# Output products that wait chunk by chunk, rotated parts first, and the context's product at the head of the second block

## The chip, the cores and the metric

The kernel runs on one core of one Trainium2 chip. The time is device microseconds of one execution. Three runs of the kernel before gave 3758.86, 3758.86 and 3766.8 us, median 3758.86 us. The profiled execution took 3765.87 us, and its span, from its first to its last instruction, 3764.2 us.

## The reference, cut to what matters

Two transformer blocks run one after the other on 256 tokens of width 1024, in fp32. The first has four layers: latent attention (layers 0 and 3), stick-breaking attention (layer 1) and retention (layer 2), each followed by a feed-forward part. The second has two layers with a context of 256 more tokens, each ending in a mixture of 64 experts.

```python
# latent attention: q has a plain part (128 per head) and a rotated part (64 per head)
q = (rms_norm(q_lat, q_norm) @ w_q_up).reshape(b, s, MLA_HEADS, MLA_NOPE + MLA_ROPE)
q = jnp.concatenate([q_nope, apply_rope(q_pe, cos, sin)], axis=-1)
kv = (rms_norm(kv_lat, kv_norm) @ w_kv_up).reshape(b, s, MLA_HEADS, MLA_NOPE + MLA_V)
k_pe = apply_rope(k_pe[:, :, None, :], cos, sin)
o = blocked_causal_softmax(q, k, v, (MLA_NOPE + MLA_ROPE) ** -0.5)
return o.reshape(b, s, MLA_HEADS * MLA_V) @ w_out
# retention: a norm, a gate, then the output product
o = o * lax.rsqrt(jnp.mean(o * o, axis=-1, keepdims=True) + EPS)
o = (jax.nn.silu(g) * (o.reshape(b, s, hv) * gn_g)) @ w_out
# second block, first layer: both sets of tokens meet the same weights
h  = x * (1.0 + sc1) + sh1
hc = ctx * (1.0 + csc1) + csh1
f, q, k, v = jnp.split(h @ w_in, cuts, axis=-1)
fc, qc, kc, vc = jnp.split(hc @ w_in, cuts, axis=-1)
```

## The kernel before, in words

Activations lie with the width on the 128 partitions, as 8 chunks of 128 rows by 256 tokens. Weights come from HBM in pieces of 1 MB through a ring of 8 slots (`ring<-stream_in`), which SyncE loads in a fixed order. A slot is given back by the first matmul on the piece behind it (`take`, `piece_used`), so the loads run up to seven pieces ahead. A second stream brings the weights of the modulation vectors (`mod_stream_in`); VectorE multiplies these itself, in L1730 and L1733. In layer 0's latent attention SyncE loads them too, each half piece when VectorE is through with the one two before it.

Each engine has its own list of instructions, written out in the program, and works it off in that order. They meet in semaphores: a PSUM bank has one for "filled" and one for "drained" (`bank`, `wait_filled`, `wait_drained`), and a table `PLAN` names the bank of each product. Nothing is reordered at run time, so an engine whose next instruction waits does nothing.

Five places matter here.

- Latent attention, `mla` (layers 0 and 3). TensorE multiplies by four groups of weights: the plain query part (8 outputs of 256 columns, L709), the key part (L817), the values (L824) and the query's rotated part (4 outputs, L709). Then a fixed matrix `rot` turns the query's rotated part (L837) and the shared key's (L840). ScalarE copies queries and values out of PSUM (L1408), VectorE the keys (L1699). The rotation itself is sine products on VectorE (L1899 to L1902), the key's sum and its two masked copies there too (L1903 to L1907), and cosine products and sums of the query on GpSimd (L2403, L2405). Attention begins when all that is done. In layer 0 VectorE has two modulation pieces between these steps, and TensorE turns their results (L721) before the first scores.
- The output products `mix_out` of latent and stick-breaking attention (`pair`, L746). Before, TensorE waits until every head's output has been copied, then multiplies.
- Retention's output product (L709). Head by head, VectorE takes a reciprocal (L1982) and multiplies four chunks by it (L1984), then GpSimd multiplies those four chunks by the gate in one instruction of 1024 columns (L2439). TensorE waits for all four heads.
- The head of the second block, `fourier_gqa`. VectorE modulates the latent tokens (L2009), GpSimd the context's (L2451). `token_major` multiplies tokens by the first weight piece: first the latent tokens, then the context's.
- `attention`, the loop over heads and query blocks, whose first score follows the wait in `mla`.

## Time and profile before

| | |
|---|---|
| median of three runs | 3758.86 us (3758.86 to 3766.8) |
| profiled execution | 3765.87 us |
| its span | 3764.2 us |
| mean granted TensorE clock | 0.953 |
| TensorE busy | 3329.9 us, 88% |
| VectorE busy | 1402.9 us, 37% |
| ScalarE busy | 504.7 us, 13% |
| GpSimd busy | 425.3 us, 11% |

The profile names an engine (PE is TensorE, DVE is VectorE, ACT is ScalarE, POOL is GpSimd, SP is SyncE), a line of the program and the tiles that an instruction writes and reads. An fp32 matmul stands as two records, so "x16" on TensorE is eight matmuls of the program. The span falls into the first block (to about 1820 us), the second block's first layer (to about 2880 us) and its second layer. A bracket at the end of a row is the time the engine sat idle before it, and the instruction that ended this.

### The profile page before, as it was taken

The numbers are of one execution on the slowest core, as the hardware profiler recorded it, in microseconds if no ns is written. First come the engines' busy times: TensorE is split into PE (matmuls) and PEld (weight loads), VectorE is DVE, ScalarE is ACT, GpSimd is POOL, SyncE is SP. The second block draws the span as 40 slices with busy tenths as digits, with TensorE's granted clock in tenths as the row PEclk, the third lists the DMA queues.
The fourth block names the chain that finished last, engine by engine and source line by source line (L and its number), as shares of the span: only waits on it lengthen the run. The fifth ranks groups of instructions, "written<-read, shape, count | busy, mean of one in ns | idle before, by whom it ended". The sixth has DMA issues, their size and how long they took to land.

```text
span 3764.2 us, 40279 instructions
## 1 busy us (share of the span) xinstructions
PE 3329.9 (88%) x14228; PEld 2238.3 (59%) x14228; DVE 1402.9 (37%) x3085; ACT 504.7 (13%) x1021; POOL 425.3 (11%) x478
## 2 busy tenths in 40 slices
PE   3799897998999997889898897999894998999998
PEld 2678785887887886778664533434442676333333
DVE  7555615565013564574363322222213033111112
ACT  1210012000011002100031211111111021111111
POOL 0010102001000000000210311111112002000000
PEclk9899999999999999999999899999997999999999
DMA  7467532774434762366200479999994214998994
GB/s 291 179 240 283 225 135 89 291 274 160 157 111 180 290 268 90 135 245 234 100 34 12 164 255 349 384 376 376 363 368 145 101 59 175 382 388 367 414 369 188
DMA packets 136152, 870.05 MB, mean 231 GB/s; under 512 B 19248, under 2 KB 22448, under 8 KB 38448
## 3 DMA queue, kind: packets, MB, share of 16 engines
q1 hardware_dynamic: 94528, 675.32, 45.5%
q0 software_dynamic: 39984, 190.35, 15.5%
q8 instruction: 100, 1.64, 0.2%
q10 hardware_dynamic: 1472, 2.18, 0.2%
q14 instruction: 68, 0.56, 0.0%
HBM read 849.95 MB, written 36.18 MB: 235 GB/s over the span
## 4 chain that ended last, share of the span: by engine, by line
PE 71%; DMA 13%; DVE 8%; issue 4%; ACT 1%; POOL 1%; SPq 0%; DVEq 0%; POOLq 0%; ACTq 0%
PE ps L709 15%; PE ps L990 12%; PE ps L1230 10%; PE ps L973 9%; DMA ring<-stream_in 9%; PE ps L746 8%; PE ps L1252 6%; PE ps L1268 3%; DMA moe_out<-arena,slot_out 2%; DMA arena<-mod_stream_in 2%; PE ps L1199 2%; PE ps L735 1%; DVE arena L1733 1%; PE ps L1167 1%; DVE YS L1835 1%
## 5 line engine op out<-in xcount | busy, mean ns | idle before, releaser
L1230 PE MATMUL ps<-ring,arena 128*64 128x512 f32 (+2 forms) x2112 | 618.0, 630 | 79.2 <-DMA ring<-stream_in 79.2
L1733 DVE SCALAR_TENSOR_TENSOR arena<-arena,cond 128x512 f32<-128x512 f32 x630 | 447.6, 748 | 72.7 <-DMA arena<-mod_stream_in 62.7
L1230 PEld LDWEIGHTS ps<-ring,arena 128*64 128x64 f32 (+2 forms) x2112 | 224.7, 157 | 413.4 <-issue 411.6
L973 PE MATMUL ps<-H,ring 128*128 128x256 f32 x2048 | 453.9, 383 | 14.3 <-ACT H L1430 14.3
L990 PE MATMUL ps<-arena,ring 128*128 128x256 f32 x2048 | 445.9, 380 | 4.3 <-DVE arena L1995 4.3
L973 PEld LDWEIGHTS ps<-H,ring 128*128 128x128 f32 x2048 | 391.8, 193 | 68.2 <-issue 15.7
L990 PEld LDWEIGHTS ps<-arena,ring 128*128 128x128 f32 x2048 | 389.4, 191 | 56.6 <-issue 5.0
L1252 PE MATMUL ps<-ring,arena 128*64 128x512 f32 (+2 forms) x1056 | 314.4, 611 | 17.3 <-DMA ring<-stream_in 9.3
L1408 ACT ACTIVATE arena<-ps 128x512 f32<-128x512 f32 (+2 forms) x359 | 182.7, 509 | 861.3 <-PE ps L709 347.5
L2201 DVE TENSOR_TENSOR arena<-arena,ps 128x256 f32<-128x256 f32 x83 | 35.0, 421 | 653.3 <-ACT arena L1627 653.3
L746 PE MATMUL ps<-H,ring 128*128 128x256 f32 x1024 | 230.1, 389 | 24.5 <-ACT H L1430 14.3
L1699 DVE COPY arena<-ps 128x128 f32<-128x128 f32 (+2 forms) x153 | 74.2, 486 | 433.1 <-PE ps L709 192.9
L746 PEld LDWEIGHTS ps<-H,ring 128*128 128x128 f32 x1024 | 199.9, 196 | 55.0 <-issue 26.8
L1252 PEld LDWEIGHTS ps<-ring,arena 128*64 128x64 f32 (+2 forms) x1056 | 105.1, 152 | 193.4 <-issue 178.6
L709 PE MATMUL ps<-ring,H 128*128 128x256 f32 (+1 forms) x864 | 190.9, 388 | 26.4 <-DVE H L2009 26.4
L709 PEld LDWEIGHTS ps<-ring,H 128*128 128x128 f32 x864 | 168.8, 208 | 49.8 <-issue 29.4
L2392 POOL DMA_DIRECT2D arena<-mod_stream_in x120 | 63.8, 532 | 867.2 <-DVE arena L1733 860.8
L709 PE MATMUL ps<-arena,ring 128*128 128x256 f32 (+1 forms) x496 | 140.8, 447 | 14.1 <-POOL arena L2439 8.3
L2510 POOL DMA_INDIRECT arena<-moe_in,slot_token x83 | 84.1, 1013 | 542.5 <-DVE slot_token L2188 497.4
L2552 POOL DMA_INDIRECT moe_out<-arena,slot_out x50 | 80.0, 1600 | 546.8 <-DVE arena L2264 390.5
L709 PEld LDWEIGHTS ps<-arena,ring 128*128 128x128 f32 x496 | 97.6, 198 | 57.0 <-issue 32.1
L709 PE MATMUL ps<-arena 128*128 128x128 f32 (+2 forms) x608 | 121.3, 343 | 10.3 <-POOL arena L2405 5.9
(251 smaller groups left out, 3054.6 us busy)
## 6 DMA issues: line engine op xcount, KB each, us to landing
ring<-stream_in SPq DMA_DIRECT2D x618, 1024.0 KB, 9.2
arena<-mod_stream_in POOLq DMA_DIRECT2D x120, 1024.0 KB, 5.1
arena<-mod_stream_in SPq DMA_DIRECT2D x12, 1024.0 KB, 7.3
YS<-mod_stream_in SPq DMA_DIRECT2D x12, 1024.0 KB, 4.9
moe_out<-zeros POOLq DMA_DIRECT2D x10, 256.0 KB, 3.0
moe_in<-YS POOLq DMA_DIRECT2D x1, 2048.0 KB, 7.6
moe_out<-arena POOLq DMA_DIRECT2D x1, 2048.0 KB, 9.3
YS<-moe_out POOLq DMA_DIRECT2D x1, 2048.0 KB, 18.9
```

The lines of the kernel that those rows point to most:

```text
L709: m = mm(out, lhs, rhs, start=(i == 0), stop=(i == len(pairs) - 1))
L746: m = mm(out[:, i * T:(i + 1) * T], w[:, off + c * width + i * P:off + c * width + i * P + P], r, start=(c == 0), stop=(c == len(rhs) - 1))
L973: m = mm(out[:, i * T:(i + 1) * T], w[:, c * 256 + i * P:c * 256 + i * P + P], h_lat[c], start=(c == 0), stop=(c == DC - 1))
L990: m = mm(out[:, i * T:(i + 1) * T], w[:, c * P:(c + 1) * P], f_h[:, 16 * half + c, :], start=(half == c == 0), stop=(half == 1 and c == 15))
L1199: m = nc.tensor.transpose(out[:, c * P:(c + 1) * P], e_x[:, k % 2, at:at + P], ident)
L1230: m = mm(out[at, :], e_xt[:, k % 2, 4 * part + c, at], w[:, c * TC:(c + 1) * TC], start=(part == c == 0), stop=(part == 1 and c == 3))
L1252: m = mm(out[at, :], e_ht[:, c, at], w[:, c * D + half * 512:c * D + (half + 1) * 512], start=(c == 0), stop=(c == 1))
L1268: m = mm(ps[:, 2 * tb + half, :], t_spread[:, k % 2, tb * P:(tb + 1) * P], e_y[:, k % 2, half * 512:(half + 1) * 512], start=False, stop=( ...
L1408: return fn(out, in_(ps[:, b, :]), func, **kw).then_inc(drained[b], 1)
L1733: ins = stt(acc, w, x, acc, MUL, ADD)
L2510: pool.indirect_dma_start(e_x[:, k % 2, :], None, h2[0:cols], bass.IndirectOffsetOnAxis(slot_token[:, at:at + 1], 0), bounds_check=cols - ...
L2552: pool.indirect_dma_start(ff, bass.IndirectOffsetOnAxis(slot_out[:, at:at + 1], 0), e_y[:, k % 2, :], None, compute_op=ADD).then_inc(scatt ...
```

## The change

It has three parts.

1. *Output products.* The wait for all chunks of the input is gone. The first of each product's outputs waits before each chunk for that chunk alone: for a head's two query blocks (latent attention), a pair of heads (stick-breaking), two chunks of four of a head (retention). For the last, GpSimd's gate is cut into eight instructions of 512 columns instead of four of 1024.
2. *Latent attention.* The query's rotated part is multiplied first, the `rot` products come between the plain ones, and VectorE does its rotations before it copies the keys; in layer 0 the second of the modulation pieces there now comes behind both. The ring piece with the rotated part's weights is taken first but given back last.
3. *Second block.* The context's product comes ahead of the latent one, and their banks change places.

```diff
-                for k in range(2 * MLA_H):
-                    wait_drained(pe, PLAN["att", l], 3 * k + 2)
+                def wait_head(h):
+                    for qb in range(2):
+                        wait_drained(pe, PLAN["att", l], 3 * (2 * h + qb) + 2)
                 for k in range(4):
-                    pair(ph, k, k, [m_o[:, h, :] for h in range(MLA_H)])
+                    pair(ph, k, k, [m_o[:, h, :] for h in range(MLA_H)], waits=None if k else wait_head)
...
-                for g in range(8):
-                    wait_drained(pe, ph, 5 * g + 4)
-                ph = PLAN["mix_out", l]
+                mixed, ph = ph, PLAN["mix_out", l]
                 for k in range(4):
-                    pair(ph, k, k, [s_o[:, c, :] for c in range(8)])
+                    pair(ph, k, k, [s_o[:, c, :] for c in range(8)], waits=None if k else lambda c: wait_drained(pe, mixed, 5 * c + 4))
...
-                pe.wait_ge(ret_gated, RET_H)
...
-                                 full if i else None, used)
+                                 full if i else None, used, None if k or i else lambda c: pe.wait_ge(ret_gated, c // 2 + 1))
...
-                token_major(ph, 0, 0, (0, 1), wait_latent(0))
-                token_major(ph, 1, 0, (2, 3), wait_context(0))
+                token_major(ph, 0, 0, (2, 3), wait_context(0), True)
+                token_major(ph, 1, 0, (0, 1), wait_latent(0), False)
...
-                for h in range(RET_H):
-                    pool.wait_ge(ret_normed, 4 * h + 4)
-                    at = slice(4 * h, 4 * h + 4)
+                for h in range(2 * RET_H):
+                    pool.wait_ge(ret_normed, 2 * h + 2)
+                    at = slice(2 * h, 2 * h + 2)
                     g.tensor_tensor(r_o[:, at, :], r_o[:, at, :], r_g[:, at, :], MUL).then_inc(ret_gated, 1)
```

The new order of latent attention on TensorE (of the old lines only the changed ones stand here):

```diff
+                w, _ = take(ph, 2)
+                for k in range(2):
+                    out, full = bank(ph, k)
+                    for i in range(2):
+                        n = (2 * k + i) * P
+                        products(out[:, i * T:(i + 1) * T], [(w[:, c * 512 + n:c * 512 + n + P], qlat[c]) for c in range(2)],
+                                 full if i else None)
+                w, used = take(ph, 0)
+
+                def rotated_key():
+                    out, full = bank(ph, 4)
+                    mm(out[:, 0:T], rot, m_kpe, start=True, stop=True).then_inc(full, 1)
+
+                def rotated(k):
+                    wait_drained(pe, ph, k)
+                    out, full = bank(ph, 2 + k)
+                    for i in range(2):
+                        m = mm(out[:, i * T:(i + 1) * T], rot, m_qp[:, 2 * k + i, :], start=True, stop=True)
+                    m.then_inc(full, 1)
+
                 for k in range(4):
-                    w, used = take(ph, 0)
-                    out, full = bank(ph, k)
+                    out, full = bank(ph, 5 + k)
...
+                    if k < 2:
+                        rotated(k)
+                    elif k == 2:
+                        rotated_key()
...
-                for k in range(12):
+                for k in range(5, 17):
                     wait_drained(pe, ph, k)
                 pe.wait_ge(mla_rope, 2 * j + 2)
                 pe.wait_ge(kpe_ready, 2 * j + 2)
...
-                attention(l, beside if l == 0 else None)
+                attention(l, beside if l == 0 else None, take(ph, 2)[1])
```

TensorE's own order in layer 3, from the last value product to the first scores of attention, before. A name in brackets is a semaphore that the instruction waits for; `piece_full` is a landed ring piece, `drained` a copied-out bank.

```order
L824 MATMUL ps<-ring,arena 128x512 [waits drained7]
L709 MATMUL ps<-arena,ring 128x256 [waits drained0,piece_full7]
L709 MATMUL ps<-arena,ring 128x256 x3
L709 MATMUL ps<-arena,ring 128x256 [waits drained1]
L709 MATMUL ps<-arena,ring 128x256 x3
L837 MATMUL ps<-arena,tab 128x256 [waits drained2,drained0]
L837 MATMUL ps<-arena,tab 128x256
L837 MATMUL ps<-arena,tab 128x256 [waits drained3,drained1]
L837 MATMUL ps<-arena,tab 128x256
L840 MATMUL ps<-arena,tab 128x256 [waits drained4]
```

Now, from the first product after the query's norm:

```order
L709 MATMUL ps<-arena,ring 128x256 [waits drained4,piece_full7,mla_lat]
L709 MATMUL ps<-arena,ring 128x256 x3
L709 MATMUL ps<-arena,ring 128x256 [waits drained5]
L709 MATMUL ps<-arena,ring 128x256 x3
L709 MATMUL ps<-arena,ring 128x256 [waits drained1,piece_full5]
L709 MATMUL ps<-arena,ring 128x256 x3
L824 MATMUL ps<-arena,tab 128x256 [waits drained6,drained4]
L824 MATMUL ps<-arena,tab 128x256
L709 MATMUL ps<-arena,ring 128x256 [waits drained2]
L709 MATMUL ps<-arena,ring 128x256 x3
L824 MATMUL ps<-arena,tab 128x256 [waits drained7,drained5]
L824 MATMUL ps<-arena,tab 128x256
```

The `rot` products (L837 before, L824 in the new numbering) moved from the end of the group to its first third, each with four plain matmuls between it and the copy that it needs; the values' products are now the last thing ahead of the scores.

TensorE from retention's last mean square to its output product, before and then now:

```order
L709 MATMUL ps<-YS,tab 128x256 [waits drained5,ret_sq]
L709 MATMUL ps<-YS,tab 128x256 x3
L709 MATMUL ps<-arena,ring 128x256 [waits piece_full3,drained0,ret_gated]
L709 MATMUL ps<-arena,ring 128x256 x15
L709 MATMUL ps<-arena,ring 128x256 [waits piece_full4]
```

```order
L709 MATMUL ps<-YS,tab 128x256 [waits drained5,ret_sq]
L709 MATMUL ps<-YS,tab 128x256 x3
L709 MATMUL ps<-arena,ring 128x256 [waits ret_gated,piece_full3,drained0]
L709 MATMUL ps<-arena,ring 128x256 [waits ret_gated] x15
L709 MATMUL ps<-arena,ring 128x256 [waits piece_full4]
```

The one wait for the gates became sixteen, a chunk each.

TensorE at the head of the second block, before and then now:

```order
L709 MATMUL ps<-ring,H 128x256 [waits hm_dve,drained0,piece_full4]
L709 MATMUL ps<-ring,H 128x256 [waits hm_dve] x7
L709 MATMUL ps<-ring,H 128x256 x8
L709 MATMUL ps<-ring,H 128x256 [waits hm_pool,drained1,piece_full4]
L709 MATMUL ps<-ring,H 128x256 [waits hm_pool] x7
L709 MATMUL ps<-ring,H 128x256 x8
```

```order
L709 MATMUL ps<-ring,H 128x256 [waits hm_pool,drained0,piece_full4]
L709 MATMUL ps<-ring,H 128x256 [waits hm_pool] x7
L709 MATMUL ps<-ring,H 128x256 x8
L709 MATMUL ps<-ring,H 128x256 [waits hm_dve,drained1,piece_full4]
L709 MATMUL ps<-ring,H 128x256 [waits hm_dve] x7
L709 MATMUL ps<-ring,H 128x256 x8
```

The sixteen matmuls on the context, which wait for GpSimd (`hm_pool`), now stand ahead of the sixteen that wait for VectorE (`hm_dve`).

## Rows read from the trace of the kernel before

**Rows 1.** The page: span and busy times; DMA issues, KB each, median us to landing.

```profile
span 3764.2 us, 40279 instructions
...
YS<-mod_stream_in SPq DMA_DIRECT2D x12, 1024.0 KB, 4.9
```

**Rows 2.** Timeline of TensorE, layer 3: start us, length us, instruction, [idle <-releaser].

```profile
1466.70 8.86 PE L709 MATMUL ps<-arena,ring 128*128 128x256 f32 x32 [2.30 <-DVE arena L1883]
...
1487.55 0.59 PE L840 MATMUL ps<-arena,tab 128*128 128x256 f32 x2
1494.05 3.76 PE L709 MATMUL ps<-arena 128*128 128x128 f32 x12 [5.91 <-POOL arena L2405]
```

**Rows 3.** Timeline of the other engines in the same stretch.

```profile
1479.05 0.69 DVE L1699 COPY arena<-ps 128x512 f32<-128x512 f32 x1 [0.17 <-PE ps L817]
...
1489.61 1.37 DVE L1905 TENSOR_TENSOR arena<-arena 128x256 f32<-128x256 f32 x1
...
1485.93 0.60 ACT L1408 ACTIVATE arena<-ps 128x512 f32<-128x512 f32 x1 [1.13 <-PE ps L709]
...
1492.44 1.26 POOL L2405 TENSOR_TENSOR arena<-arena 128x512 f32<-128x512 f32 x1
```

**Rows 4.** Timeline of VectorE and TensorE, layer 0.

```profile
91.09 0.48 DVE L1730 TENSOR_SCALAR stat<-YS,cond 128x512 f32<-128x512 f32 x1
...
101.72 5.54 DVE L1733 SCALAR_TENSOR_TENSOR stat<-YS,cond,stat 128x512 f32<-128x512 f32 x7
...
112.57 1.50 DVE L1907 TENSOR_SCALAR arena<-arena,vec 128x256 f32<-128x256 f32 x2
...
115.72 1.94 PE L721 MATMUL ps<-tab,stat 128*128 128x128 f32 x8 [6.02 <-POOL arena L2405]
```

**Rows 5.** Timeline of TensorE, start of two output products (layers 0 and 1).

```profile
166.30 27.87 PE L746 MATMUL ps<-arena,ring 128*128 128x256 f32 x128 [0.69 <-DVE arena L1699]
...
606.70 27.87 PE L746 MATMUL ps<-arena,ring 128*128 128x256 f32 x128 [0.82 <-DVE arena L1699]
```

**Rows 6.** Timeline around retention's gates: TensorE, VectorE, GpSimd.

```profile
1096.90 4.00 PE L709 MATMUL ps<-YS,tab 128*128 128x256 f32 x16
...
1109.16 11.09 PE L709 MATMUL ps<-arena,ring 128*128 128x256 f32 x43 [8.26 <-POOL arena L2439]
...
1101.13 1.67 DVE L1984 SCALAR_TENSOR_TENSOR arena<-arena,vec,stat 128x256 f32<-128x256 f32 x4
1104.50 2.19 DVE L1984 SCALAR_TENSOR_TENSOR arena<-arena,vec,stat 128x256 f32<-128x256 f32 x4
...
1102.88 2.34 POOL L2439 TENSOR_TENSOR arena<-arena 128x1024 f32<-128x1024 f32 x1 [1.99 <-DVE arena L1984]
1106.77 2.34 POOL L2439 TENSOR_TENSOR arena<-arena 128x1024 f32<-128x1024 f32 x1 [1.55 <-DVE arena L1984]
```

**Rows 7.** The chain that ended last, retention's output product.

```profile
1109.16 57.06 PE ps L709 x256
```

**Rows 8.** Timeline at the head of the second block: TensorE, VectorE, GpSimd.

```profile
1818.21 3.62 PE L735 MATMUL ps<-YS,tab 128*128 128x256 f32 x16
1831.36 16.31 PE L709 MATMUL ps<-ring,H 128*128 128x256 f32 x64 [9.53 <-DVE H L2009]
1847.50 4.88 PE L709 MATMUL ps<-H,ring 128*128 128x512 f32 x11
...
1830.80 3.82 DVE L2009 TENSOR_SCALAR H<-X,scale,mod 128x256 f32<-128x256 f32 x8
...
1819.98 4.31 POOL L2451 TENSOR_SCALAR H<-X,scale,mod 128x256 f32<-128x256 f32 x8 [24.43 <-DVE scale L1787]
```

**Rows 9.** Stretches from:to us; busy us of each engine, granted clock (PEclk), DMA.

```profile
1466.00:1470.00 4.00, 3.30 (x9) 2.73 (x10) 2.79 (x4) 0.03 (x1) 0.00 (x0) 0.66 0.34 82
1831.00:1835.00 4.00, 3.64 (x9) 2.95 (x10) 3.62 (x8) 0.00 (x0) 3.62 (x3) 0.50 0.35 70
```

**Rows 10.** Timeline of SyncE's queue, loads of the expert weights.

```profile
2111.70 76.15 SPq L665 DMA_DIRECT2D ring<-stream_in  x12
```

More of the change, by code:

```diff
@@ L750, in pair, with token_major @@
                 m.then_inc(full, 1)
-            def token_major(ph, k, j, blocks, waits=None):
+            def token_major(ph, k, j, blocks, waits=None, first=None):
                 w, used = take(ph, j)
@@ L758, in token_major @@
                              [(H[:, c, tb * P:(tb + 1) * P], w[:, c * 256:(c + 1) * 256]) for c in range(DC)],
-                             full if i == 1 else None, used if i == 0 and blocks[0] == 0 else None, None if i else waits)
+                             full if i == 1 else None, used if i == 0 and (blocks[0] == 0 if first is None else first) else None, None if i else waits)
             def wait_h(s):
@@ L772, in attention @@
                         out, full = bank(ph, 3 * i)
-                        products(out[:, 0:units[i]["nk"]], units[i]["score"], full)
+                        products(out[:, 0:units[i]["nk"]], units[i]["score"], full, None if i else used)
                     if 2 <= i < len(units) + 2:
@@ L814, in mla @@
                 for k in range(4):
-                    out, full = bank(ph, 4 + k)
+                    out, full = bank(ph, 9 + k)
                     for i in range(2):
@@ L821, in mla @@
                 for k in range(4):
[L822 removed]
+                    out, full = bank(ph, 13 + k)
                     tb, half = k // 2, k % 2
[L824 to L837 removed]
+                    m = mm(out, m_klat[:, tb * P:(tb + 1) * P], w[:, D + half * 512:D + (half + 1) * 512], start=True, stop=True)
                     m.then_inc(full, 1)
[L839 to L841 removed]
+                for k in range(5, 17):
                     wait_drained(pe, ph, k)
@@ L1471, in mla @@
                 ph = PLAN["mla_up", l]
-                for k in range(0, 4):
-                    drain(ph, k, m_qn[:, 2 * k:2 * k + 2, :], pairs)
-                for k in range(8, 12):
-                    tb, half = (k - 8) // 2, k % 2
-                    drain(ph, k, m_v[:, tb, half * 512:(half + 1) * 512], whole)
-                for k in range(12, 14):
-                    drain(ph, k, m_qp[:, 2 * (k - 12):2 * (k - 12) + 2, :], pairs)
+                for k in range(2):
+                    drain(ph, k, m_qp[:, 2 * k:2 * k + 2, :], pairs)
+                for k in range(4):
+                    drain(ph, 5 + k, m_qn[:, 2 * k:2 * k + 2, :], pairs)
+                for k in range(4):
+                    tb, half = k // 2, k % 2
+                    drain(ph, 13 + k, m_v[:, tb, half * 512:(half + 1) * 512], whole)
                 attention(l)
@@ L1890, in mla @@
                     mod_pair(1)
-                for k in range(4, 8):
-                    drain(ph, k, m_kn[:, 2 * (k - 4):2 * (k - 4) + 2, :], pairs)
-                if l == 0:
-                    mod_pair(2)
                 dve.wait_ge(rope_ready, 2)
@@ L1907, in mla @@
                     ts(m_kpm[:, i, :], m_t1[:, 2, :], V("parity", i), None, MUL).then_inc(kpe_ready, 1)
+                for k in range(4):
+                    drain(ph, 9 + k, m_kn[:, 2 * k:2 * k + 2, :], pairs)
+                if l == 0:
+                    mod_pair(2)
                 s, n, _ = ph.piece(2)
```

31 lines of the change are left out of this document (7 added, 24 removed).

## Prediction

> **What bounds the kernel now.** I read the page first, to see which engine carries the span: TensorE is busy for most of it, the others for a third or less, so time is to be had only where TensorE stands still. Then the chain that ended last and TensorE's own waits, in the stretches that the change touches; there a reader is to see which other engine released TensorE after each gap. Last the timelines of those other engines, to see what would be late next, and the granted clock after each gap. The span is 3764.2 us [rows 1]; the profiled execution took 3765.87 us, 7.0 us (0.19%) more than the median of the runs shown, 3758.86 us. The sum below is made against 3765.87.
>
> The gaps of TensorE that the change can reach are 5.91 us ahead of layer 3's attention [rows 2], 6.02 us in layer 0 [rows 4], 0.69, 0.82 and once more 0.69 us (layer 3) ahead of three output products [rows 5], 8.26 us ahead of retention's [rows 6] and 9.53 us at the head of the second block [rows 8]. Together 31.9 us. Nothing is added to TensorE: the number of matmuls is the same. A matmul of 256 columns takes 0.43 us at the full clock: sixteen records, eight matmuls, start to end 3.62 us, of which the last is about 0.17 us of modelled tail [rows 8], and 57.06 us for retention's 128, which hold 1.8 us of slow start over 128 x 0.4317 = 55.25 [rows 7].
>
> **Latent attention, layer 3.** Before, TensorE is through at 1488.14 (1487.55 + 0.59) and waits until GpSimd's last sum, 1492.44 + 1.26 = 1493.70, to start at 1494.05 [rows 2, 3]. In the new order the rotated part's eight matmuls start at 1466.70 and end near 1471.9, as the first four matmuls run at half clock (the granted clock is 0.66 from 1466 to 1470) [rows 9]. The `rot` products come at about 1473.7 and 1476.3, the key's at 1478.9. The second pair's sine products end near 1478.2; GpSimd needs about 3.0 us per pair (1.7 for two cosine products, 1.26 for the sum [rows 3]) and is done near 1481.6. VectorE's chain for the key, four steps that took 4.1 us in all before, ends near 1483.7; its four copies of keys, 0.69 us each [rows 3], near 1486.5. TensorE does the same work as before and is through at 1488.1. What is late next is ScalarE's copy of the last value bank: 0.15 us to see it, 0.60 us for the copy [rows 3], and the step to TensorE: scores at about 1489.05. Gain 1494.05 - 1489.05 = **5.0 us**. Bounds: 4.0 if ScalarE's table load for the exponential, which moves behind that copy, no longer hides; 6.3 if, with the gap gone, the first scores also run at full clock (twelve records in 3.76 us [rows 2] against some 2.5).
>
> **Latent attention, layer 0.** Here VectorE is the one that fills up. It has two modulation pieces of about 6.1 us (5.54 for seven of the eight steps of the second [rows 4]), the copies, and the rotation. From the first piece's start at 91.09 to the end of the key's masks, 112.57 + 1.50 = 114.07, are 22.98 us [rows 4], of which it waited some 2.5 us for TensorE, so 20.5 us of work. In the new order I count 2.4 us of such waits, now for the `rot` products, so it ends near 114.0 again, but with the second modulation piece. TensorE's transposes need that piece, so they start at 114.0 instead of 115.72: **1.7 us**, not the 6.02 of the gap. Queued behind the waiting transposes are the scores; behind VectorE's piece are two sums that the transposes feed. The next half pieces are loaded when VectorE is through with the second pair: issued near 110.9 and 114.0, landing 4.9 us later [rows 1] at 115.8 and 118.9, needed near 117.0 and 120.3. This hides with 1.2 us to spare; a landing 3 us late would eat the gain. Bounds 0 and 2.4.
>
> **Output products of attention.** TensorE's last product of the last head is followed at once by chunk 0, and seven chunks of 0.43 us cover the copy of the last head. Gain 0.7 + 0.8 + 0.7 = **2.2 us** [rows 5] (bounds 1.6 and 2.8, as waits split per chunk can cost or save a tenth each).
>
> **Retention.** The mean squares end at 1096.90 + 4.00 = 1100.9 [rows 6]; chunk 0 starts there. Chunks 0 to 7 (heads 0 and 1) are gated by then and take 3.5 us. Head 2: VectorE starts its four products at 1101.13, two of them done at 1102.0, GpSimd gates these in about 1.2 us (half of 2.34, and 1.26 was seen for 512 columns [rows 3, 6]). Here a cost comes in. VectorE's four products take 1.67 us when GpSimd is idle, but 2.19 us where GpSimd's gate of 1102.88 to 1105.22 overlaps their start at 1104.50 [rows 6]: VectorE's instruction with two inputs waits for GpSimd's to end. In the new order GpSimd is at work on the first half while VectorE does the fourth chunk, in every head. So I let that chunk end 0.3 us after GpSimd's half: head 2 gated at 1103.3 and 1104.9, VectorE's reciprocal for head 3 ends at 1105.2 instead of 1104.5, its first two products at 1106.05, GpSimd's halves at 1107.3 and 1108.9. Chunks 14 and 15 then end near 1109.9. The other 112 matmuls at full clock take 48.35 us: end 1158.3. Before, the product ended at 1109.16 + 56.9 = 1166.1 [rows 7]. Gain **7.8 us**. Bounds: 8.9 if the engines share without loss; 4.0 if each half costs 2.34 us and the product's two short gaps bring the slow start back (2.0 and 1.8).
>
> The Trainium skill, "GPSIMD Engine Reference", section "Specifications", says that GpSimd's SBUF interfaces are shared with VectorE and contend with VectorE instructions that have two SBUF inputs. By that rule, the trace agrees: the products overlapped take 2.19 us instead of 1.67. Without it this term would be 8.9; I keep 7.8.
>
> **Second block.** Mean square's last matmuls end near 1821.8 [rows 8]. GpSimd modulates the context from 1819.98 to 1824.29, 0.54 us a chunk; TensorE's first eight matmuls follow it and the second eight end near 1828.5. The latent tokens' product starts at 1831.36, when VectorE's first chunk is there (1830.80, 0.48 us a chunk [rows 8]): eight paced by VectorE, 3.8 us, eight of 0.43 us, 3.5 us, end 1838.7. Before, both products together ran to 1847.50 [rows 8]. That would be 8.8 us. But before, 16.14 us for 32 matmuls hold 2.3 us of half clock (0.50 granted from 1831 to 1835 [rows 9]), and a gap of about 2.9 us remains now. In layer 3 a gap of 2.30 us was followed by a granted clock of 0.66 [rows 2, 9]. So part comes back: I take **7.6 us**, bounds 8.8 and 4.5 (the context's sixteen matmuls at half clock, 13.8 us, would end at 1835.7). ScalarE's copies are in the same order as the products.
>
> No load is moved in SyncE's or GpSimd's list. Slots of the ring are given back at other moments: the key weights' slot some 7 us later in layer 3, under 26 us of attention that takes nothing from the ring; without that cover it would be one load late.
>
> **The sum.** 5.0 + 1.7 + 2.2 + 7.8 + 7.6 = 24.3 us. Every later stage keeps its distance: the experts' loads of the second block start only behind the routing (2111.70 [rows 10]). Against the profiled execution 3765.9 - 24.3 = 3741.6; against the median 3758.86 - 24.3 = **3734.6 us**. Low terms give 4.0 + 0 + 1.6 + 4.0 + 4.5 = 14.1, high ones 6.3 + 2.4 + 2.8 + 8.9 + 8.8 = 29.2.
>
> **Rivals.** (a) *The next engine takes most of it*: the modulation half piece lands late in layer 0, GpSimd's halves cost as much as its wholes, and every shortened gap still brings half clock. For it: the half clock behind a gap of 2.30 us. Against: 56.9 us of retention's product had only one such start. The low terms: 3758.9 - 14 = 3745 us.
>
> (b) *A stream paces a later stage*, so an earlier start is given back, above all among the experts, where TensorE waits for `ring<-stream_in`. For it: that stage runs on loads. Against: its loads are issued only after routing, so they move with it. All of it lost: 3759 us.
>
> (c) *Slower: the chunk waits hold TensorE at half clock.* The place is retention's output product: with short gaps between chunks instead of one long one, the granted clock might stay at 1.2 GHz over the whole product, 55.25 us more, less the 24.3: 3759 + 31 = 3790 us. It decides from 24 us on, 44% of that product at half clock. Against: the pre-norm's products wait chunk by chunk already, and after the second block's first 4 us at 0.50 the same product goes on at full speed [rows 8, 9].
>
> The Trainium skill, "TensorE: Matmul & The Clock Gate", section "A second HAM failure mode: psum-queue depth-cycling", tells of a kernel whose short idle moments between groups of matmuls made the clock go back and forth between its levels. By that rule (c) would hold; the trace shows no such stretch here, and (c) keeps a small chance.
>
> (d) *The change doesn't do what it says*, if GpSimd came to the context late. It doesn't: its eight instructions end at 1824.29, 7 us before the latent tokens' [rows 8]. I give it nothing.
>
> **How the numbers follow.** Forecast (a gain of 19 to 29 us) 0.72, (a) 0.15, (b) 0.07, (c) 0.06. What a measurement of this kernel can tell from no change is about 0.2%, 7.5 us. Faster: 0.72 + 0.15 = 0.87; the same 0.07; slower 0.06. The range runs from 3758.9 - 29.2 less a little for waits of a tenth, 3728, to (a)'s 3745 with most of the 7 us by which single runs of the kernel before differ: 3750.
>
> **What would show it.** Scores of layer 3 about 1 us behind the last value product, released by ScalarE; layer 0's transposes released by VectorE's modulation step; retention's product starting right behind the mean squares, with two short waits for GpSimd; VectorE's gate products longer than 1.67 us in every head; a context product of 7 us and a gap near 3 us at the head of the second block. The forecast is wrong if a gap of the old size stands anywhere, or if the expert stage grows.

## The result, and the profile after

| | before | after |
|---|---|---|
| median of six runs each | 3767.49 us (3758.86 to 3770.87) | 3740.76 us (3733.13 to 3747.71) |
| ratio of times, 95% interval | | 0.9932 (0.9913 to 0.995) |
| span of the profiled execution | 3764.2 us | 3740.7 us |
| mean granted clock | 0.953 | 0.955 |

The change makes the kernel 0.68% faster, with an interval of 0.5 to 0.87%. Of 3767.49 us that is 25.6 us; the spans differ by 23.5 us. The forecast was 3734.6 us, 24.3 us below the median of three then known, and the measured 3740.76 us lies in its range. The six runs of the kernel before have a median 8.6 us above that of the first three, so a fair comparison is of the differences: 24.3 us foreseen, 25.6 by the ratio of the medians, 23.5 us between the profiled spans.

To see where they come from I cut both traces on TensorE, at the mean square behind each attention and each feed-forward part. Stage by stage, in us:

| stage | before | after | difference | foreseen |
|---|---|---|---|---|
| layer 0, latent attention | 133.51 | 129.14 | -4.37 | -2.4 |
| layer 0, feed-forward | 256.69 | 261.40 | +4.71 | 0 |
| layer 1, stick-breaking | 183.72 | 182.89 | -0.83 | -0.8 |
| layer 1, feed-forward | 256.73 | 256.86 | +0.13 | 0 |
| layer 2, retention | 274.92 | 268.14 | -6.78 | -7.8 |
| layer 2, feed-forward | 261.53 | 261.56 | +0.03 | 0 |
| layer 3, latent attention | 122.08 | 114.99 | -7.09 | -5.7 |
| layer 3, feed-forward | 268.54 | 266.54 | -2.00 | 0 |
| head of the second block | 29.29 | 21.83 | -7.46 | -7.6 |

The rows add to -23.7 us; the products of 512 columns that follow start at 1823.89 instead of 1847.50 [rows 8], 23.61 us earlier, and the 1917 us behind them are as long as before (1916.8 against 1916.7). That these two agree is partly luck. No kernel of this document has other instructions there, and the same stretch took 1904.9 to 1918.9 us in the twelve other profiles, 1912.9 in a second one of the kernel after. So medians move by some us on their own, and the stages are the better measure.

Timeline of TensorE in the kernel after, layer 3, then the head of the second block (start us, length us, instruction, [idle <-releaser]):

```profile
1477.40 3.60 PE L849 MATMUL ps<-ring,arena 128*128 128x512 f32 x8
1482.20 1.99 PE L709 MATMUL ps<-arena 128*128 128x128 f32 x12 [1.20 <-ACT arena L1417]
...
1802.06 3.62 PE L735 MATMUL ps<-YS,tab 128*128 128x256 f32 x16
1805.52 7.07 PE L709 MATMUL ps<-ring,H 128*128 128x256 f32 x32
1815.23 8.83 PE L709 MATMUL ps<-ring,H 128*128 128x256 f32 x32 [2.64 <-DVE H L2018]
```

The 5.91 us of [rows 2] are down to 1.20 us, and ScalarE's last copy has taken GpSimd's place as the releaser. At the head of the second block 2.64 us are left of 9.53 [rows 8], and the context's product takes 7.07 us, which is full clock. The latent one takes 8.83, partly at half clock: the granted clock there, beside that of layer 3, is

```profile
1815.00:1819.00 4.00, 3.77 (x10) 3.09 (x11) 3.49 (x8) 0.00 (x0) 3.75 (x3) 0.57 0.00 0
1459.00:1463.00 4.00, 3.36 (x9) 2.74 (x10) 2.73 (x4) 0.13 (x1) 0.00 (x0) 0.66 0.00 0
```

(Columns as in [rows 9], the clock third from the end.)

Retention's output product in the kernel after, timeline of TensorE, then of VectorE and GpSimd:

```profile
1096.59 4.00 PE L709 MATMUL ps<-YS,tab 128*128 128x256 f32 x16
1100.43 4.48 PE L709 MATMUL ps<-arena,ring 128*128 128x256 f32 x20
1105.28 1.13 PE L709 MATMUL ps<-arena,ring 128*128 128x256 f32 x4 [0.37 <-POOL arena L2448]
1108.03 1.13 PE L709 MATMUL ps<-arena,ring 128*128 128x256 f32 x4 [1.62 <-POOL arena L2448]
1109.65 15.59 PE L709 MATMUL ps<-arena,ring 128*128 128x256 f32 x71 [0.49 <-POOL arena L2448]
```

```profile
1101.20 2.68 DVE L1993 SCALAR_TENSOR_TENSOR arena<-arena,vec,stat 128x256 f32<-128x256 f32 x4
1103.80 1.74 DVE L1991 RECIPROCAL stat<-stat 128x256 f32<-128x256 f32 x1
1105.58 2.68 DVE L1993 SCALAR_TENSOR_TENSOR arena<-arena,vec,stat 128x256 f32<-128x256 f32 x4
...
1102.15 1.45 POOL L2448 TENSOR_TENSOR arena<-arena 128x512 f32<-128x512 f32 x1 [1.31 <-DVE arena L1993]
...
1106.54 1.44 POOL L2448 TENSOR_TENSOR arena<-arena 128x512 f32<-128x512 f32 x1 [1.31 <-DVE arena L1993]
1108.34 1.26 POOL L2448 TENSOR_TENSOR arena<-arena 128x512 f32<-128x512 f32 x1 [0.36 <-DVE arena L1993]
```

One gap of 8.26 us [rows 6] has become three of 0.37, 1.62 and 0.49 us. VectorE's four products, 1.67 us in [rows 6], now take 2.68 or 2.69 us in every head, because GpSimd's first half runs beside them; the one-input reciprocal keeps its 1.74 us.

One row of the table was not foreseen: layer 0's feed-forward part is 4.71 us longer, though nothing in it was changed. Timeline of TensorE there, before:

```profile
212.97 14.05 PE L973 MATMUL ps<-H,ring 128*128 128x256 f32 x64 [3.56 <-ACT H L1430]
...
358.82 1.09 PE L721 MATMUL ps<-tab,arena 128*128 128x128 f32 x8 [1.91 <-DVE route_s L1747]
```

and after:

```profile
209.00 16.72 PE L982 MATMUL ps<-H,ring 128*128 128x256 f32 x64 [3.56 <-ACT H L1439]
...
357.52 1.78 PE L721 MATMUL ps<-tab,arena 128*128 128x128 f32 x8 [1.91 <-DVE route_s L1756]
359.10 28.83 PE L999 MATMUL ps<-arena,ring 128*128 128x256 f32 x128
```

The gaps are the same, 3.56 and 1.91 us. What differs is the work behind them: 16.72 instead of 14.05, 1.78 instead of 1.09, and the product behind it 28.83 instead of the 27.79 us it takes before and elsewhere, 4.4 us together. The stretches say why (before, then after):

```profile
213.00:217.00 4.00, 4.00 (x19) 3.54 (x20) 3.89 (x9) 2.62 (x7) 0.00 (x0) 1.00 0.47 164
358.00:362.00 4.00, 3.18 (x19) 2.93 (x20) 3.29 (x9) 0.00 (x0) 0.00 (x0) 1.00 0.35 104
```

```profile
209.00:213.00 4.00, 4.00 (x10) 3.19 (x11) 3.92 (x9) 2.65 (x7) 0.00 (x0) 0.50 0.36 106
357.00:361.00 4.00, 3.48 (x13) 3.12 (x14) 2.86 (x8) 0.00 (x0) 0.00 (x0) 0.60 0.15 57
```

The granted clock is 0.50 and 0.60 after the same gaps that left it at 1.00 before: 1.2 GHz instead of 2.4 at first.

Layer 3's feed-forward part went the other way. The first product behind the same gap, before and after:

```profile
1568.35 15.74 PE L973 MATMUL ps<-H,ring 128*128 128x256 f32 x64 [3.57 <-ACT H L1430]
1554.35 14.05 PE L982 MATMUL ps<-H,ring 128*128 128x256 f32 x64 [3.56 <-ACT H L1439]
```

That is 1.69 of its 2.00 us.

### The profile page after: what moved, and what is told of

The parts are those of the page before. It is cut to its first block, busy times and chain, and to the rows that moved or that the text cites. A ratio compares the mean times of both kernels' runs of the same rounds, so it can differ in the third digit from the quotient of the medians.

```text
span 3740.7 us, 40275 instructions
## 1 busy us (share of the span) xinstructions
PE 3328.8 (89%) x14228; PEld 2231.6 (60%) x14228; DVE 1403.1 (38%) x3085; ACT 504.6 (13%) x1021; POOL 427.4 (11%) x482
## 4 chain that ended last, share of the span: by engine, by line
PE 72%; DMA 13%; DVE 9%; issue 4%; ACT 1%; POOL 0%; SPq 0%; POOLq 0%; DVEq 0%; ACTq 0%
PE ps L709 14%; PE ps L999 12%; PE ps L1239 10%; PE ps L982 9%; PE ps L746 8%; DMA ring<-stream_in 8%; PE ps L1261 6%; PE ps L1277 3%; DMA arena<-mod_stream_in 2%; PE ps L1208 2%; DMA moe_out<-arena,slot_out 2%; PE ps L735 1%; DVE arena L1742 1%; PE ps L1176 1%; DVE YS L1844 1%
## 5 line engine op out<-in xcount | busy, mean ns | idle before, releaser
L999 PEld LDWEIGHTS ps<-arena,ring 128*128 128x128 f32 x2048 | 389.5, 191 | 57.6 <-issue 5.0
L721 PE MATMUL ps<-tab,arena 128*128 128x128 f32 x360 | 55.8, 292 | 83.0 <-DVE arena L1742 66.8
L1277 PE MATMUL ps<-arena,YS 128*128 128x512 f32 x264 | 128.9, 612 | 0.0
```

Of the source, the lines that this page charges most:

```text
L999: m = mm(out[:, i * T:(i + 1) * T], w[:, c * P:(c + 1) * P], f_h[:, 16 * half + c, :], start=(half == c == 0), stop=(half == 1 and c == 15))
L1277: m = mm(ps[:, 2 * tb + half, :], t_spread[:, k % 2, tb * P:(tb + 1) * P], e_y[:, k % 2, half * 512:(half + 1) * 512], start=False, stop=( ...
```

## The experiments

All times are medians beside runs of the kernel before on the same chip; a ratio is to these.

**The parts alone.** Four kernels are the kernel before with one piece of the change each. They ask whether the terms stand by themselves, and which of them carries the 4.7 us of loss.

Only the chunk waits of latent and stick-breaking attention. 

> Only the chunk waits of the output products of latent and stick-breaking attention. Theory: 0.7 to 0.8 us at each of three places, 2.2 us in all, not to be told from no change by the time; in the profile no gap ahead of the three products. Rival (the waits split per chunk slow the first output): the products take 1 us or more longer each, with small gaps between matmuls, and the time is the same or worse.

```diff
-                    pair(ph, k, k, [m_o[:, h, :] for h in range(MLA_H)])
+                    pair(ph, k, k, [m_o[:, h, :] for h in range(MLA_H)], waits=None if k else wait_head)
...
-                    pair(ph, k, k, [s_o[:, c, :] for c in range(8)])
+                    pair(ph, k, k, [s_o[:, c, :] for c in range(8)], waits=None if k else lambda c: wait_drained(pe, mixed, 5 * c + 4))
```

Measured 3763.98 us, ratio 0.9995 (0.9982 to 1.0009): nothing that can be told. In the trace the gap ahead of layer 0's output product is gone:

```profile
167.51 0.68 PE L709 MATMUL ps<-arena 128*128 128x128 f32 x4 [0.40 <-ACT arena L1408]
168.03 12.25 PE L746 MATMUL ps<-arena,ring 128*128 128x256 f32 x56
```

and layers 1 and 3 are 0.85 and 0.91 us shorter, as foreseen; but layer 0's attention is 1.75 us longer (its first product, behind a gap of 3.57 us, took 15.74 us there and 14.05 before) and its feed-forward part 4.5 us.

Only the new order of latent attention, part 2 of the change. 

> Only latent attention's new order, its output product still waiting for all heads. Theory: the scores of layer 3 start 5.0 us earlier behind the query's norm than before, those of layer 0 about 3.8; 9 us less in all if the half-clock starts of layer 0's feed-forward part don't fall worse than before, 5 us if they do as in the changed kernel's profile. Rival (layer 0 gives its gain back by something that the new order itself causes, as a late load): layer 0's feed-forward part is longer again by 3 to 5 us, with waits for loads.

```diff
...
+                w, _ = take(ph, 2)
+                for k in range(2):
...
+                    if k < 2:
+                        rotated(k)
+                    elif k == 2:
+                        rotated_key()
...
```

3751.79 us, 0.9961 (0.9948 to 0.9975). Layer 3 gives 6.17 us, layer 0's attention 2.07, layer 3's feed-forward 1.61, and layer 0's feed-forward loses 3.04.

Only retention's half gates and waits. 

> Only the retention part of the change: its output product waits chunk by chunk, the gate is cut into eight halves. Theory (each part gives the gap it removes, in its own stage): 7 us less from the last mean square to the end of retention's output product, two gaps of about 1.5 us for GpSimd inside the first output, VectorE's four products 2.7 us a head; the other stages as before, so 7 us (0.19%) less in all, give or take 3 us of half-clock starts that fall differently. Rival (the gain came from where the half-clock starts fall over the whole program, not from this wait): the stage gains under 3 us.

```diff
-                pe.wait_ge(ret_gated, RET_H)
...
-                                 full if i else None, used)
+                                 full if i else None, used, None if k or i else lambda c: pe.wait_ge(ret_gated, c // 2 + 1))
...
-                for h in range(RET_H):
-                    pool.wait_ge(ret_normed, 4 * h + 4)
-                    at = slice(4 * h, 4 * h + 4)
+                for h in range(2 * RET_H):
+                    pool.wait_ge(ret_normed, 2 * h + 2)
+                    at = slice(2 * h, 2 * h + 2)
```

3759.15 us, 0.9977 (0.9958 to 0.9996). Retention gives 5.71 us, 1.07 less than in the whole change. The gaps inside its product are the same, but here half clock follows the one of 1.62 us:

```profile
1114.00:1118.00 4.00, 4.00 (x11) 2.81 (x12) 0.12 (x1) 0.00 (x0) 1.26 (x1) 0.57 0.00 0
```

Layer 0's attention is 2.64 us longer than before, and here too the feed-forward part of layer 0 takes 259.78 us instead of 256.69, in a program whose instructions up to its end are those of before. So the loss needs neither the new order nor the new waits, and TensorE's gaps there show no wait for a load.

Only the second block. 

> Only the second block's part: the context's product first. Theory: the two products end 7.5 us earlier behind the mean square than before, with a gap of 2.6 us between them and some half clock behind it; 7 us (0.2%) less in all. Rival (the half clock behind the gap takes it back): under 4 us.

```diff
-                token_major(ph, 0, 0, (0, 1), wait_latent(0))
-                token_major(ph, 1, 0, (2, 3), wait_context(0))
+                token_major(ph, 0, 0, (2, 3), wait_context(0), True)
+                token_major(ph, 1, 0, (0, 1), wait_latent(0), False)
...
-                    drain(ph, k, a_f[:, 2 * k:2 * k + 2, :], pairs)
+                    drain(ph, k, a_f[:, 2 * (1 - k):2 * (1 - k) + 2, :], pairs)
```

3754.92 us, 0.997 (0.9955 to 0.9985), some 11 us by the ratio; in the trace the head is 7.46 us shorter, exactly as in the whole change, layer 0's feed-forward part takes 256.59 us as before (256.69), and the stretch behind the head, which nothing changes, is 4.0 us shorter.

**Gates in whole heads.** 

> The changed kernel, but with retention's gate in four whole instructions again; the output product waits chunk by chunk for whole heads. Theory (VectorE's products and GpSimd's gate exclude each other, so halves gain little): VectorE's four products take 1.67 us again in three heads of four, the last gate ends at 8.2 us behind the last mean square, and retention's stage is 0.5 us longer than with halves. Rival (the halves themselves are what gains, 1.9 us less wait for the last chunk): 2 us longer.

```diff
-                                 full if i else None, used, None if k or i else lambda c: pe.wait_ge(ret_gated, c // 2 + 1))
+                                 full if i else None, used, None if k or i else lambda c: pe.wait_ge(ret_gated, c // 4 + 1))
...
-                for h in range(2 * RET_H):
-                    pool.wait_ge(ret_normed, 2 * h + 2)
+                for h in range(RET_H):
+                    pool.wait_ge(ret_normed, 4 * h + 4)
```

This is the kernel after with GpSimd's four instructions of 1024 columns back. 3738.64 us, 0.9923 (0.99 to 0.9946); retention 268.21 us against 268.14. Timeline of TensorE and, last row, of VectorE:

```profile
1106.62 2.00 PE L709 MATMUL ps<-arena,ring 128*128 128x256 f32 x8 [0.93 <-POOL arena L2448]
1110.51 15.81 PE L709 MATMUL ps<-arena,ring 128*128 128x256 f32 x72 [1.89 <-POOL arena L2448]
...
1102.47 1.67 DVE L1993 SCALAR_TENSOR_TENSOR arena<-arena,vec,stat 128x256 f32<-128x256 f32 x4
```

The halves gain nothing. What they save in waiting, VectorE pays: its products take 1.67 us here (2.20 in the last head) and 2.68 there. All of the 6.8 us comes from TensorE's no longer waiting for all heads.

**Gates ahead of the norm.** A head's gate need not wait for its reciprocal, as both are factors. GpSimd gates each head as soon as its squares are taken, and VectorE's product, now last, releases TensorE chunk by chunk. 

> The changed kernel, but GpSimd multiplies by the gate before VectorE's norm instead of behind it, as soon as the squares are taken (the factors are the same, in another order), and the output product waits for VectorE's products chunk by chunk. Theory (the end of the stage is VectorE's and GpSimd's work in a row): GpSimd's gates lie beside the mean squares, TensorE has no gap left ahead of or in the first output, and the stage is 3.0 us shorter than in the changed kernel, up to 4 with the half clock gone; 10 us shorter than before in all. Rival (GpSimd's gates now stop VectorE's products, as they share the port): VectorE's products are stretched by as much, under 1 us gained.

```diff
-                for h in range(2 * RET_H):
-                    pool.wait_ge(ret_normed, 2 * h + 2)
-                    at = slice(2 * h, 2 * h + 2)
+                for h in range(RET_H):
+                    pool.wait_ge(ret_sq, h + 1)
+                    at = slice(4 * h, 4 * h + 4)
...
+                        dve.wait_ge(ret_gated, h + 1)
...
-                                 full if i else None, used, None if k or i else lambda c: pe.wait_ge(ret_gated, c // 2 + 1))
+                                 full if i else None, used, None if k or i else lambda c: pe.wait_ge(ret_normed, c + 1))
```

3733.78 us, 0.9913 (0.9884 to 0.9941); once more beside other kernels 3731.02 us, 0.9894 (0.987 to 0.9917). TensorE, VectorE and GpSimd:

```profile
1100.48 25.85 PE L709 MATMUL ps<-arena,ring 128*128 128x256 f32 x119
...
1104.25 1.67 DVE L1994 SCALAR_TENSOR_TENSOR arena<-arena,vec,stat 128x256 f32<-128x256 f32 x4
...
1098.67 2.36 POOL L2449 TENSOR_TENSOR arena<-arena 128x1024 f32<-128x1024 f32 x1 [1.99 <-ACT YS L1540]
```

No gap is left, VectorE is back at 1.67 us, and retention takes 264.84 us, 3.3 less than after and 10.1 less than before. 

> gate_first once more, as what keep_busy_gf is compared with on the same chip. Both theories: the same time within 0.2%; the retention stage again 3.3 us shorter than in the changed kernel. Theory on the clock: layer 0's feed-forward part and the first products of the stages differ by up to 3 us each from the first profile, though the program is the same.

The repeat has the same stages within 0.1 us (264.85 for retention), but for layer 0's attention, 130.52 against 129.08. There the first product, behind the same gap, took this long in the first profile and in the second:

```profile
69.66 14.05 PE L746 MATMUL ps<-H,ring 128*128 128x256 f32 x64 [3.57 <-ACT H L1439]
70.17 16.83 PE L746 MATMUL ps<-H,ring 128*128 128x256 f32 x64 [3.57 <-ACT H L1439]
```

The granted clock at its start was 1.00 and then 0.50, in one and the same program.

**Is the half clock of layer 0's feed-forward part chance?** The same kernel after, profiled once more. 

> The changed kernel once more, a second profile of the same program. Theory (half-clock starts fall by chance): the gaps and releasers stand where they stood, but layer 0's feed-forward part, 261.4 us from mean square to mean square in the first profile and 256.7 before the change, may take any value between. Rival (the new order makes that part slower): 261 us again.

3738.48 us (one execution), and the stage took 261.41 us again (261.40 the first time). All five profiles of kernels that hold the whole change and no spare matmuls (below), the two of `gate_first` and that of `gate_whole` among them, lie between 261.26 and 261.43. So at this place it came back with the program, which is what the rival said, though not by the rival's cause: `only_retention`, without the new order, has most of the loss. It is no rule for every place: layer 0's attention fell both ways in the two profiles of `gate_first`.

**Filling TensorE's gaps.** If half clock follows idle time, matmuls whose result nobody reads should take it away where they fit into a gap. They are added to the kernel before and to the kernel after, in each layer of the first block behind two mean squares, that of the norm ahead of the attention and that of the norm ahead of the feed-forward part:

```diff
+            def spare_products(n):
+                for _ in range(n):
+                    mm(ps[:, 4, 0:T], ones_d, ax_cos, start=True, stop=True)
...
+                spare_products(7)
```

> The kernel before with only the seven idle-time matmuls behind each mean square ahead of a layer's or feed-forward part's first product. Theory (they level the half clock in the feed-forward parts): layer 0's feed-forward part stays near 257 us, where it was with little half clock already; the layers where it took 261.5 us come down to 258; 4 to 8 us less in all than the kernel before. Rival: no difference from the kernel before.

3749.84 us, 0.9958 (0.9945 to 0.9972), faster than the kernel before though it does more, and by more than was expected. Not all of that can be put down to the filled gaps: in the profiles 8.5 us lie ahead of the second block's 512-column products (1838.96 against 1847.50 [rows 8]), and 10.5 us behind them, where nothing was filled and where profiles differ on their own. 

> The changed kernel with the same seven matmuls at the same places, to be set against before_busy: the change with the half clock of the feed-forward parts levelled. Theory (layer 0's gain of 4.4 us was given back by half clock only): layer 0's feed-forward part takes 257 us instead of 261.4, and the change is worth 28 us against before_busy, 4 to 5 more than the 23.5 between the first two profiles. Rival (it was given back by something of the new order): 261 us again, and 23.5 us between the two.

3719.01 us, 0.9882 (0.9853 to 0.9911). Timeline of TensorE in this kernel at layer 0's feed-forward, and its clock:

```profile
205.00 3.19 PE L730 MATMUL ps<-tab 128*128 128x256 f32 x14
208.73 14.05 PE L986 MATMUL ps<-H,ring 128*128 128x256 f32 x64 [0.54 <-ACT H L1445]
```

```profile
209.00:213.00 4.00, 4.00 (x20) 3.51 (x19) 3.89 (x9) 2.39 (x6) 0.00 (x0) 1.00 0.63 190
```

The gap of 3.56 us is 0.54, the first product takes 14.05 us again and the stage 257.16.

Eight such products stand in the first block, each behind a gap of 3.56 or 3.57 us. In the ten profiles without spare matmuls 23 of these 80 took 14.05 us, and the other 57 took 15.6 to 16.8. In the four filled ones (two more follow below) all 32 took 14.05.

With both programs filled alike, the starts of the second block's 512-column products lie 28.7 us apart (1838.96 and 1810.27), where they were 23.6, so between the filled kernels the change is worth 28.7 us; the medians say 30.8. Of the 5.1 us more, 3.9 come from layer 0's feed-forward part, which is the half clock given back. Another 2.9 come from layer 0's attention, where `before_busy` was 2.6 us slower than the kernel before (its output product took 30.28 us, not 27.87 [rows 5]), and the other stages take 1.8 off again.

**More of it.** The kernel with gates ahead of the norm, the seven spare matmuls and five more between the context's and the latent product. 

> The kernel of gate_first with seven matmuls of no use behind each mean square ahead of a layer's or feed-forward part's first product, and five between the second block's context and latent products; they write a bank that nobody reads. Theory (the half clock at the start of a stage comes from TensorE's idle time before it, and where it falls is chance): the first products of the eight stages take 14.0 us each instead of 14.0 to 16.7, the latent product 7.3 instead of 8.8; 5 to 8 us less in all than gate_first. Rival (the level doesn't follow such short work, or the extra matmuls delay what waits): the first products are as slow as before, the time is the same or some us more.

```diff
                 token_major(ph, 0, 0, (2, 3), wait_context(0), True)
+                for _ in range(5):
+                    mm(ps[:, 4, 0:T], ones_d, ax_cos, start=True, stop=True)
                 token_major(ph, 1, 0, (0, 1), wait_latent(0), False)
```

3721.86 us, 0.9872 (0.985 to 0.9893). Timeline of TensorE at the head of the second block:

```profile
1787.14 7.07 PE L709 MATMUL ps<-ring,H 128*128 128x256 f32 x32
1794.05 2.32 PE L1045 MATMUL ps<-tab 128*128 128x256 f32 x10
1796.85 7.47 PE L709 MATMUL ps<-ring,H 128*128 128x256 f32 x32 [0.48 <-DVE H L2027]
```

The latent product takes 7.47 us instead of 8.83. It starts 9.71 us behind the context's product as in the kernel after, and its granted clock is now 1.00 from the start, so the clock was what made it long.

Then twelve more behind the mean squares that follow the attention and the feed-forward part (not the last layer's). 

> keep_busy_gf with twelve more such matmuls behind each mean square that ends a layer or a feed-forward part, where TensorE waits 5.5 us. Theory: the next mean square's first eight records take 1.9 us instead of 3.75, but the rest of it waits for VectorE as before, so 0.5 us at each of seven places, 3 us in all less than keep_busy_gf. Rival (that gap brings half clock into what follows as well): 10 us less.

```diff
+                spare_products(12)
...
+                if l < DEPTH - 1:
+                    spare_products(12)
```

3723.01 us, 0.9891 (0.9862 to 0.992): no gain over the last, and neither number came true. Layer 0's transposes behind the unfilled 1.91 us gap are at half clock here:

```profile
353.80 1.85 PE L721 MATMUL ps<-tab,arena 128*128 128x128 f32 x8 [1.91 <-DVE route_s L1767]
```

The three filled kernels with the change in them, 3719 to 3723 us, can't be told apart, and all their medians lie below those of the kernels before and after; of those without spare matmuls `gate_first`, 3731 and 3734 us, is the best.

## Why the prediction was right, and where it was not

**Layer 3** (5.0 + 0.7 foreseen, 7.09 measured). The mechanism was right to the releaser: GpSimd's last sum ended at 1473.09 + 1.33, before the key products were even done, and the scores started 1.20 us after the values, released by ScalarE's last copy. From the first product's start to the scores it now takes 1482.20 - 1459.64 = 22.56 us, before 27.35 [rows 2]: 4.8 us against 5.0. The first twelve score records took 1.99 us instead of 3.76 [rows 2], the upper bound's case: behind this gap no half clock is seen (granted 1.00 from 1481 to 1485). Term and bound together make 6.3; 6.17 in the kernel with this part alone.

**Layer 0** (1.7 + 0.7 foreseen, 4.37 measured). The step that failed is the count of VectorE's work. Timelines of VectorE in the kernel before, then of VectorE and of TensorE in the kernel after:

```profile
110.30 0.83 DVE L1903 TENSOR_TENSOR arena<-arena,rope 128x256 f32<-128x256 f32 x1
111.17 1.37 DVE L1905 TENSOR_TENSOR arena<-arena 128x256 f32<-128x256 f32 x1
```

```profile
101.25 0.49 DVE L1908 TENSOR_TENSOR arena<-arena,rope 128x256 f32<-128x256 f32 x1
101.78 0.83 DVE L1910 TENSOR_TENSOR arena<-arena 128x256 f32<-128x256 f32 x1
...
107.22 5.55 DVE L1742 SCALAR_TENSOR_TENSOR stat<-YS,cond,stat 128x512 f32<-128x512 f32 x7
...
110.69 0.63 PE L721 MATMUL ps<-tab,stat 128*128 128x128 f32 x4 [1.20 <-DVE stat L1742]
112.82 1.11 PE L721 MATMUL ps<-tab,stat 128*128 128x128 f32 x4 [1.50 <-DVE stat L1742]
113.72 2.77 PE L709 MATMUL ps<-arena 128*128 128x128 f32 x8
```

I took VectorE's 20.5 us of work as unchanged and ended at 114.0; VectorE was done at 107.22 + 5.55 = 112.8. The key's cosine product took 0.49 us instead of 0.83 and its sum 0.83 instead of 1.37, which is most of it; why is not shown, as in layer 3 the sum kept its 1.37. And that the transposes wait for the whole piece ("so they start at 114.0") was wrong too: four of the eight records need only half of it and ran from 110.69, so the scores came 0.9 us behind VectorE's end and not 1.7 (115.72 [rows 4] to 117.45 before). The scores start at 113.72 and the output product at 160.90 instead of 166.30 [rows 5]. That product then took 28.94 us, not 27.87, which is why the stage gave 4.37 and not 5.4.

**Output products** (2.2). Layers 1 and 3 gave 0.83 and 0.9, as foreseen. Layer 0's gap went too. Alone this part moved the median by nothing that can be told, as expected of 2.2 us; in its trace layer 0's feed-forward part took 4.5 us more.

**Retention** (7.8, measured 6.78). That VectorE's products would be longer than 1.67 us in every head came true, and so did the 0.3 us by which the fourth chunk ends behind GpSimd's half (1101.20 + 2.68 = 1103.88 against 1102.15 + 1.45 = 1103.60). The term was mis-sized by what stands around them. I let VectorE start head 2 where it did before, 1101.13 - 1096.90 = 4.23 us behind the start of the last mean square [rows 6], but heads 0 and 1 had been stretched already: it was 1101.20 - 1096.59 = 4.61. And GpSimd's first half took 1.45 us, not 1.2. I had the last chunks done 9.0 us after the product's start; the matmuls behind them started at 1110.62, which is 10.2, and 0.2 of these are an earlier start. Rival (a)'s bound, halves at the price of wholes (2.34 us), did not come; but `gate_whole` shows that cutting the gates in halves gained nothing either.

**Second block** (7.6, measured 7.46). Context product 7 us, gap 2.9 and some half clock behind it were foreseen; 7.07, 2.64 and a clock of 0.57 were found.

**What stood nowhere.** The sum hit 24.3 by 23.7 because errors in both directions cancel, which is luck: the two attention stages gave 3.4 us more than foreseen and layer 3's feed-forward part 2.0, which nobody had counted, retention 1.0 less, and layer 0's feed-forward part took 4.7. "Every later stage keeps its distance" is true of the loads and false of the clock. These are stretches of it in both kernels, each a whole feed-forward part, layer 0's and layer 3's, before:

```profile
194.00:450.69 256.69, 240.68 (x1137) 210.11 (x1136) 151.31 (x241) 19.60 (x35) 20.55 (x36) 0.99 0.69 262
1549.67:1818.21 268.54, 247.18 (x1154) 214.33 (x1152) 167.23 (x281) 19.07 (x35) 16.11 (x28) 0.97 0.60 219
```

and after:

```profile
189.68:451.08 261.40, 245.38 (x1138) 213.26 (x1136) 151.43 (x241) 19.61 (x35) 20.62 (x36) 0.97 0.68 257
1535.52:1802.06 266.54, 244.55 (x1153) 212.00 (x1152) 167.28 (x281) 19.06 (x35) 16.17 (x28) 0.98 0.60 221
```

VectorE, ScalarE and GpSimd did the same work within 0.2 us; the clock went from 0.99 to 0.97 in one and from 0.97 to 0.98 in the other. Rival (a) named this kind of loss, but where the gaps were shortened. It stood at gaps that nobody had touched. Rival (b) fell: the second block behind its head kept its length, and in no profile was it more than 2.2 us longer. Rival (c) fell as well: behind its three short gaps retention's product runs on at full clock, two records in 0.44 us (71 in 15.59). In `only_retention` one of these gaps did bring half clock, but for a few us (0.57 from 1114 to 1118, then 1.00), not for the whole product.

What is still open is which of these gaps brings half clock. That the idle time brings it is shown by filling it, 32 products of 32 against 23 of 80. Why 3.56 us do so at one place or in one execution and not in another is not shown: up to there `only_retention` and `only_second` have the instructions of before, and took 259.78 and 256.59 us.

## What to carry to other kernels

When one long wait for all of something is split, look first at what the producers do to each other when they overlap: here half gates slowed VectorE by what they saved, and moving the gate off the last chain was worth 3.3 us more. Price each part from the wait that comes next, as was done here, but expect several us either way from clock changes in stages that the change does not touch, and compare stage by stage before you believe that a sum is right. Where TensorE has gaps of some 3.5 us before large products, a few matmuls that fit inside the gap and whose result nobody reads are a cheap trial: up to the second block's 512-column products they saved 8.5 us in the kernel before and 13.6 in the kernel after.

## What the runs showed of the hardware

- A product of two SBUF tiles on VectorE is held up by a GpSimd instruction with two inputs: four of 128x256 took 1.67 us alone, 2.19 to 2.20 us beside part of a gate, 2.68 us beside a half gate in full. The reciprocal, with one input, kept 1.74 us beside the same.
- The Trainium skill, "GPSIMD Engine Reference", section "Specifications", says that the two contend where VectorE has two SBUF inputs; these rows agree, and give the size in this kernel.
- The same gap of 3.56 or 3.57 us ahead of the same product was followed by full clock at 23 of 80 places and by half clock at first at the other 57. Of the sixteen places in two programs profiled twice, fifteen repeated the product's length within 0.02 us, and one went from 14.05 to 16.83 us.
- With the gap filled down to 0.54 us, all 32 products ran at full clock, 14.05 us.
- Shorter gaps brought half clock too: a clock of 0.57 followed 2.64 us at the head of the second block, behind a product of 7.07 us at full clock, and in `only_retention` it followed 1.62 us.
